# A two-block fp32 network on one core: the order of taps, sums, roots and weight copies around its norms

## The reference, cut

```python
def rms_norm(x, gain):
    return x * lax.rsqrt(jnp.mean(x * x, axis=-1, keepdims=True) + 1e-6) * gain

def first_block(x, ...):
    h = rms_norm(x, mix_norm_pre)
    xa, ga, q, k, v, f_logit, g_a, g_b = jnp.split(h @ w_in, offs, axis=-1)
    xc = causal_dwconv(xa, conv_a_w, conv_a_b)                 # 4 taps
    y_a = gelu(ga) * rg_lru(xc, ...)
    y_b = forgetting_attention(q, k, v, f_logit + b_forget)
    merged = (sigmoid(g_a + b_merge[0]) * (y_a @ w_proj_a)
              + sigmoid(g_b + b_merge[1]) * (y_b @ w_proj_b))
    x = x + rms_norm(merged @ w_out, mix_norm_post)
    up = causal_dwconv(rms_norm(x, ffn_norm_pre) @ w_up, conv_f_w, conv_f_b)   # 3 taps
    gate, val = jnp.split(up, 2, axis=-1)
    return x + rms_norm((gelu(gate) * val) @ w_down, ffn_norm_post)

def second_block(h, ...):
    for layer in range(2):
        y = rms_norm_2(h, norm_mix[layer])
        h = h + (hgrn2_mixer(y, ...) if layer == 0 else moba_mixer(y, ...))
        h = h + swiglu(rms_norm_2(h, norm_ffn[layer]), ffn_w13[layer], ffn_w2[layer])
    return rms_norm_2(h, final_norm)
```

## Time and profile before

| | |
|---|---|
| median of 3 runs | 1181.46 us (1181.43 to 1182.18) |
| the profiled execution | 1182.08 us, its span 1180.30 us |
| mean granted TensorE clock | 0.993 of full |
| TensorE busy (PE) | 1156.0 us, 98% of the span |
| DVE busy | 907.2 us, 77% |
| ACT busy | 711.8 us, 60% |
| POOL busy | 383.5 us, 32% |
| moved by DMA | 204.32 MB, 173 GB/s |

### The profile page before, as it was taken

How to read it: one execution, slowest core, us unless ns; L and a number is a source line. 1 busy time by engine, 2 the same in 40 slices (tenths; PEclk the granted TensorE clock), 3 DMA queues, 4 the chain that set the end, 5 groups by cost and what they waited for, 6 DMA issues and landing times.

```text
span 1180.3 us, 23771 instructions
## 1 busy us (share of the span) xinstructions
PE 1156.0 (98%) x8406; PEld 1087.2 (92%) x8406; DVE 907.2 (77%) x1365; ACT 711.8 (60%) x1142; POOL 383.5 (32%) x406
## 2 busy tenths in 40 slices
PE   8999999999999999999999999999999999999996
PEld 8999999999899999888999988888899999888886
DVE  7867897967699998548899698777666768777754
ACT  6498656545467777435755776665555556766552
POOL 2444000701445555224000145555220015554431
PEclk9999999999999999999999999999999999999999
DMA  6556434476445666662635256566765435665661
...
DMA packets 56562, 204.32 MB, mean 173 GB/s; under 512 B 6688, under 2 KB 6840, under 8 KB 56368
## 3 DMA queue, kind: packets, MB, share of 16 engines
...
## 4 chain that ended last, share of the span: by engine, by line
PE 85%; DVE 10%; ACT 3%; issue 1%; DMA 1%; POOL 0%; DVEq 0%; SPq 0%; ACTq 0%; POOLq 0%
PE bank L1450 21%; PE bank L1456 14%; PE bank L1457 14%; PE bank L1458 14%; PE bank L1451 12%; DVE w_lo L734 3%; PE bank L1453 2%; PE bank L1560 2%; PE bank L1561 2%; PE bank L1562 2%; DVE h_two L764 1%; DVE work L889 1%; DVE work L788 1%; PE bank L1647 1%; ACT w_hi L310 1%
## 5 line engine op out<-in xcount | busy, mean ns | idle before, releaser
L734 DVE TENSOR_TENSOR w_lo<-raw,w_hi 128x1024 fp32r<-128x1024 f32 x374 | 477.3, 1283 | 131.8 <-ACT w_hi L310 127.4
L310 ACT ACTIVATE w_hi<-raw 128x1024 fp32r<-128x1024 f32 x374 | 391.4, 1051 | 121.0 <-PE bank L1451 58.0
L1456 PE MATMUL bank<-h_two,w_hi 128*128 128x256 f32 x1184 | 344.1, 291 | 9.9 <-DVE h_two L764 4.9
L1457 PE MATMUL bank<-h_two,w_hi 128*128 128x256 f32 x1184 | 336.9, 285 | 0.0
L1458 PE MATMUL bank<-h_two,w_lo 128*128 128x256 f32 x1184 | 336.8, 284 | 0.0
L1456 PEld LDWEIGHTS bank<-h_two,w_hi 128*128 128x128 f32 x1184 | 228.7, 193 | 15.3 <-issue 8.3
L1457 PEld LDWEIGHTS bank<-h_two,w_hi 128*128 128x128 f32 x1184 | 229.0, 193 | 0.5
L1458 PEld LDWEIGHTS bank<-h_two,w_lo 128*128 128x128 f32 x1184 | 229.0, 193 | 0.0
L1450 PE MATMUL bank<-h_two,w_hi 128*128 128x512 f32 x616 | 221.4, 398 | 1.0 <-DVE h_two L764 1.0
L1451 PE MATMUL bank<-h_two,w_lo 128*128 128x256 f32 x704 | 183.5, 281 | 0.0
L1450 PE MATMUL bank<-u_two,w_hi 128*128 128x512 f32 x455 | 161.6, 398 | 0.0
...
## 6 DMA issues: line engine op xcount, KB each, us to landing
raw<-in_stream SPq DMA_DIRECT2D x374, 512.0 KB, 3.5
...
```

Of the source, the lines that this page charges most:

```text
L310: A(w_hi[:, slot, :], raw[:, slot, :], ACT.Copy).then_inc(hi_ready, 1)
L734: v.tensor_tensor(w_lo[:, slot, :], raw[:, slot, :], w_hi[:, slot, :].bitcast(F32), ALU.subtract).then_inc(lo_ready, 1)
L1456: mm(out, w_hi[:, slot, s], r_two[:, 0, :], start=start, stop=False)
L1457: mm(out, w_hi[:, slot, s], r_two[:, 1, :], start=False, stop=False)
```

## The change

- Transfers: the first eight columns of `par` (the first gain) go alone at the head of SP's queue, the other 377 behind part 1. POOL's five loads wait for the second half of x.
- First phase: the sum of the norm stands behind the third tile instead of the second; the table product moves ahead of tile 5. DVE makes copy 4 ahead of the first root. The taps of a pair follow the next pair's norming, with one low copy ahead of them and one behind; the last pair's taps stand in stage `v`. The high parts of the results move back likewise. The forget weights lie as one operand of 48 columns (high, high, low), so that there are 16 matmuls instead of 24, two normings and an addition; the split of these weights moves to pair 2 and the gate parameters to stage `v`.
- Roots: ACT takes the logarithm of the mean square and then the exponential of -0.5 times it, both from one table set, which is loaded where `touch` was used with Sqrt or Exp; DVE has no reciprocal.
- Behind the branches: DVE alone scales (one block, one block, then pairs as one operation of 512 columns), 14 matmuls of ones instead of 20, three tiles at once by blocks, and the squares of each block summed by TensorE itself, one matmul a block.
- Weight copies: behind both branches ACT makes the high part of the next part ahead of the root and another right behind it, and DVE two low ones ahead of its first norming. The first pass of `up` is written out ahead of the loop. A pair in `up` has one low copy ahead of its taps and one behind them. In `hf`, ACT does three sigmoids first and then alternates, and DVE's low copy is one part further ahead.

The diff, cut to its core:

```diff
@@ SP, first transfers
-            sp.dma_start(par[:, :], par_d).then_inc(par_in, 16)
+            sp.dma_start(par[:, 0:C], par_d[:, 0:C]).then_inc(gain_in, 16)
             ...
                 sp.dma_start(raw[:, n, :], stream[n]).then_inc(landed[n], 16)
+                if n == 1:
+                    sp.dma_start(par[:, C:NCOL], par_d[:, C:NCOL]).then_inc(par_in, 16)
@@ ACT, rms and table loads
-                A(RSTD, bank[4][:, 0:S], ACT.Sqrt, scale=1.0 / D, bias=der[:, D_EPS:D_EPS + 1]).then_inc(rms_ready, 1)
+                A(RSTD, bank[4][:, 0:S], ACT.Ln, scale=1.0 / D, bias=eps).then_inc(ms_log, 1)
+                act.wait_ge(ms_log, NORMS[norm] + 1)
+                A(RSTD, RSTD, ACT.Exp, scale=-0.5).then_inc(rstd_ready, 1)
+            def norm_tables():
+                act.preload_act_table_set("natural_log_exp_and_others")
-                    A(touch, touch, ACT.Sqrt)
+                    norm_tables()
@@ ACT, ahead of up
             for c in range(C):
                 split("ffn", c)
+            multiplied(PART["up"])
+            hi(0, 0, PART["up"] + HI_AHEAD)
             rms("ffn")
-            with act.Fori(0, 2 * F1 // 4) as i:
+            multiplied(PART["up"] + 1)
+            hi(0, 0, PART["up"] + 1 + HI_AHEAD)
+            def up_tiles(i, first=False):
                 A(touch, touch, ACT.Gelu_apprx_tanh)
                 ...
+            up_tiles(0, first=True)
+            with act.Fori(1, 2 * F1 // 4) as i:
+                up_tiles(i)
@@ ACT, hf
+            multiplied(PART["hf"])
+            hi(0, 0, PART["hf"] + HI_AHEAD)
             rms("n0")
+            multiplied(PART["hf"] + 1)
+            hi(0, 0, PART["hf"] + 1 + HI_AHEAD)
             for t in range(C):
                 act.wait_ge(evacuated, TILE["hf"] + t + 1)
                 A(FG_T[:, :, t, :], FG_T[:, :, t, :], ACT.Sigmoid).then_inc(f_raw, 1)
-                multiplied(PART["hf"] + t)
-                hi(0, 0, PART["hf"] + t + HI_AHEAD)
+                if t >= 2:
+                    multiplied(PART["hf"] + t)
+                    hi(0, 0, PART["hf"] + t + HI_AHEAD)
@@ DVE, rstd and add_normed
-                dve.wait_ge(rms_ready, NORMS[norm] + 1)
-                v.reciprocal(RSTD, RSTD).then_inc(rstd_ready, 1)
                 dve.wait_ge(rstd_ready, NORMS[norm] + 1)
+                scaled(0, 1)
+                added(0)
+                scaled(1, 1)
+                h_low(after, 0)
+                added(1)
+                for c in range(2, C, 2):
+                    scaled(c, 2)
+                    h_low(after, c - 1)
+                    added(c)
+                    added(c + 1)
+                    h_low(after, c)
@@ DVE, first phase
             step("xa", 0)
+            step("xa", 1)
             rstd("mix")
+            dve.wait_ge(par_in, 16)
             ...
+            for p in range(R // 2):
+                for t in (2 * p, 2 * p + 1):
+                    multiplied(PART["xa"] + t)
+                    normed(XA[:, t, :], TILE["xa"] + t)
+                if p >= 1:
+                    step("xa", 2 * p + 1)
+                if p == 2:
+                    forget_weights()
+                if p == 3:
+                    columns(1)
+                if p >= 1:
+                    taps(p - 1)
+                if 2 * p + 2 < R:
+                    step("xa", 2 * p + 2)
@@ DVE, hf
             step("hf", 0)
+            step("hf", 1)
             rstd("n0")
             for t in range(C):
                 multiplied(PART["hf"] + t)
                 normed_halves(FG_T, t, TILE["hf"] + t)
                 if t >= 1:
-                    step("hf", t)
+                    if t + 1 < C:
+                        step("hf", t + 1)
                     gate_key(t - 1)
@@ PE
+            def after_branch(norm, name, n):
+                c, t = PART[name], TILE[name]
+                def square(b):
+                    pe.wait_ge(sq_ready, C * PAIR_SUMS.index(norm) + b + 1)
+                    return mm(bank[4][:, 0:S], ones[:, :], SQ[:, b, :], start=(b == 0), stop=(b == C - 1))
+                pe.wait_ge(lo_ready, c + 3)
+                free_bank(0, 0, t + 2)
+                for b in range(BLK):
+                    pe.wait_ge(hl_ready, H_COUNT[norm] + b + 1)
+                    for j in range(3):
+                        last = three(t + j, (c + j) % RING, b, h_two[:, b, :, :], b == 0, b == BLK - 1)
+                        ...
+                    if b >= 1:
+                        square(b - 1)
+                square(C - 1).then_inc(stat_done, 1)
+                tile(0, c + 3, t + 3)
+                tiles(c + 4, t + 4, n - 4)
             tile(0, 1, 1)
+            tile(0, 2, 2)
             pair_stat("mix")
             ...
-            keep_clock(20)
-            after_norm("ffn", "up", 2 * F1)
+            keep_clock(14)
+            after_branch("ffn", "up", 2 * F1)
```

185 lines of the change are left out of this document (92 added, 93 removed).

## The result

The changed kernel takes 1185.94 us (median of 7 runs, 1184.17 to 1187.21) against 1181.46 (7 runs, 1181.32 to 1182.18): a ratio of 1.0037, 95% interval 1.0027 to 1.0046. It is slower, by 4.5 us, where no change was forecast. Its profiled execution took 1187.02 us, with a span of 1185.2. The runs also lie further apart than before, 3.0 us against 0.9; experiment 3 shows why. The profiled execution is 1.1 us above the median, so the lengths read from it hold more of what varies than a middle run does.

A forecast was written before the change was run, and what follows sets the result against it. TensorE, busy 98% of the span, was taken as the bound, with DVE equally so in the first phase. Terms 0 - 0.8 + 2.7 - 0.7 - 1.3 = -0.1 us gave 1181.4 us, range 1175.5 to 1185.5.

The forecast's parts named there:

- the signs named for being wrong: `hf` turns under 2.9 us, a start after 10.5, or TensorE's waits behind copies under 1 us in both branches.
- Second branch norm: `hf`: gain of 4.0 up to tile 3, then slower copy turns; term +2.7 us, bounds 0 and +4.3.
- The turn of 3.7 us: `hf`: DVE's copy waits for ACT's high copy made after the sigmoid, so each turn takes 3.7 us instead of 2.2.
- TensorE is 0.5 us early at `hq`, then waits longer: Behind `hf`, at `hq`: TensorE arrives 0.5 us early and then waits longer, with the halves of tile 1 +2.4.
- First branch norm: `up`: 4.0 us gained by tile 3, of which 0.8 remain after late copies; term -0.8, bounds -2.2 and +1.2.
- Tile 7's wait: `up`: tile 7 waits 2.0 us for its weight copy, which ends at 14.0 after the three tiles.
- The 0.6 at tile 6: `up`: tile 6 waits 0.6 us, in the walk of late weight copies behind the three tiles.
- the walk: `up`: DVE's chain followed step by step from the logarithm to tile 8, which starts at 346.2, before at 346.99.
- Phase one: Start to fifth token tile: earlier start offset by later root and DVE work; term 0, bounds -1.0 and +3.1.
- The other roots: `o` -0.7 us (bounds -1.35 and 0), `final` -1.3, and `f0`, `n1`, `f1` 0.
- The first, that the copies keep up: Both branches: TensorE keeps the 4.0 us; `up` alone 1178.2, `hf` alone 1174.7, both 1171.5; chance 0.23.
- Rival 2: First phase slower: later root delays DVE's chain, fifth token tile 3.1 us later if the start is unchanged, 1184.5; chance 0.14.

The follow-up runs named there:

- experiment 3: Changed kernel with TensorE's two longest waits behind the branches filled with unread matmuls of ones (7 in `up`, 12 in `hf` and `hq`): 1184.18 us.
- experiment 1: Changed kernel with ACT's high copy ahead of the sigmoid instead of behind it in `hf`: 1177.67 us.
- experiments 2: Changed kernel with both of DVE's low copies of a pair ahead of the taps in `up`'s loop: 1184.34 us.
- 5: Kernel before the change with only the roots changed, to logarithm and exponential on ACT without reciprocal: 1178.54 us.
- experiment 12: Changed kernel with old first phase but new transfers, `hf` high copy before sigmoid, `up` copies further ahead, `up1`/`up2` first copies before the root: 1169.54 us.
- 8: Changed kernel with old first phase, `hf` high copy before sigmoid, `up` copies one part further ahead, Silu's table loaded later in `up1`/`up2`: 1175.24 us.

## Why the prediction was wrong

The forecast was 1181.4 (1175.5 to 1185.5), the time 1185.94, just outside. The span grew by 4.9 us in the profiled execution where the sum had -0.1. Of these 5.0 us, 2.7 are clock (experiment 3 against the changed kernel: 2.1 in `hf` and `hq`, 0.6 in `up`), 0.8 the gain in `up` that did not come, 0.6 the roots of `f0` and `f1`, 0.6 the first phase and 0.3 the end. On the medians the clock is 1.8 of 4.5. None of the signs named for being wrong came (the turn is 3.71, the start 9.97, the waits behind copies 1.94 and 3.04); the failure lies in what the steps were priced at. By its steps:

- **Second branch norm.** Right in mechanism, wrong in size. The turn of 3.7 us was measured at 3.71, the stage at full clock at +2.83 against +2.7 forecast. The step that failed is its last sentence, "TensorE is 0.5 us early at `hq`, then waits longer": the prediction's own figures, 0.5 early and 2.4 late, make this a wait of 2.9 us, and it put no price on what follows such a wait. It came as 3.04 us at one tile, and the clock behind it costs 2.1 us more in this stage. The prediction read the half clock behind two waits of over 2 us, and counted it only where the change removes such a wait, not where it makes one.
- **First branch norm.** Tile 7's wait came out as 1.94 for 2.0. The 0.6 at tile 6 did not come, and does not follow from the walk either: three tiles of 2.88 us are 8.6, and copy 6 ends at 8.7. Of the -0.8, at most 0.4 is left at full clock (218.27 in experiment 1 and 218.67 in 3, against 218.65), because the walk ended at tile 8. At the end of `up` a TensorE that comes earlier waits for POOL's last product: 1.78 us where it was 0.46, and still 1.52 with the old order of copies (experiments 2 and 5). POOL's steps there run beside DVE's low copies. The half clock at tile 7 costs a further 0.6 to 1.0.
- **Phase one.** Term 0, measured +0.56, well within its bounds. Its last addition has a slip: 52.0 with 2.4, 2.1 and 2.4 is 58.9 and not 58.6, which is +0.4 and nearer what came. The 0 also hid two sizes: the transfers gain 2.3 us and the new order costs 3.1.
- **The other roots.** `o` -0.74 for -0.7, the end -1.03 for -1.3. For `f0` and `f1` it was argued that no wait for a root is in the trace, so 0; but what stands behind the root on ACT moves by the exponential, and the stage is 0.58 longer (477.14 in experiment 12 with the copy ahead of the root, 477.19 before).
- **Rivals.** The first, that the copies keep up, did not hold, but is what experiments 1 and 8 make true, at about its price (-3.8 and -4.1 where -4.0 was given). Rival 2 names the first phase; its condition, a start later than 11.2, did not come (9.97), and the phase lost 0.56 and not 3.1. Of the chance of slower, 0.24, half rested on rival 2; no case had the clock fall behind a new wait, which the rows of before already showed twice.

What stays open: why the clock falls behind a wait in some executions and not in others, and which of the remaining moves in the first phase costs its 1.9 us.
